# Memory projections in three rounded passes inside an attention pipeline, with VectorE's share placed in ScalarE's filling step

## The reference

```
h = RMSNorm(x);  z = h @ w_in                 # 2048 x 5944, columns shared out among two mixers
y_a = native sparse attention of z            # 8 heads of 128, 2 key/value groups
      k_cmp, v_cmp: gelu(blocks @ w1) @ w2    # 15 blocks of 32 tokens: 4096 -> 128 -> 128
y_b = RWKV-7 of z                             # 16 heads of 64
x  += concat(RMSNorm(y_a), y_b) @ w_out
m   = RMSNorm(mem);  k = m @ wk_mem;  v = m @ wv_mem       # both 2048 x 2048
x  += attention(RMSNorm(x) @ wq_mem, k, v) @ wo_mem
x  += hierarchical mixture of experts (4 groups of 8, top 2)
out = RMSNorm(x)
```

## Time and profile before

| | |
|---|---|
| runs | 1944.14, 1943.7, 1938.69 us; median 1943.7 |
| the profiled execution | 1943.37 us, its span 1941.5 us |
| busy share of the span | PE 91%, DVE 48%, ACT 34%, POOL 4% |
| mean granted TensorE clock | 0.946 of 2.4 GHz |
| the chain that ended last | PE 89%, DVE 4%, ACT 3% |
| L683 and L672 in the chain (float32 products of all units) | 20.3% and 7.4% |

### The profile page before, as it was taken

How to read it: one execution, slowest core, us unless ns; L and a number is a source line. 1 busy time by engine, 2 the same in 40 slices (tenths; PEclk the granted TensorE clock), 3 DMA queues, 4 the chain that set the end, 5 groups by cost and what they waited for, 6 DMA issues and landing times.

```text
span 1941.5 us, 28278 instructions
## 1 busy us (share of the span) xinstructions
PE 1774.4 (91%) x11978; PEld 1526.5 (79%) x11978; DVE 941.5 (48%) x1119; ACT 665.9 (34%) x709; POOL 72.6 (4%) x150
## 2 busy tenths in 40 slices
PE   6999999999989999969879789669999999998993
PEld 4887878878788888869879689668877886886882
DVE  1142423434223111143443334448878878887883
ACT  1011111101111111132333323236765765765772
POOL 4010010101010000000000000000000000000000
PEclk9899999999969999989989999769999998999997
DMA  7430605133126444416525153239977987995972
GB/s 204 143 106 9 207 11 172 53 109 115 45 94 213 131 130 130 130 69 191 173 87 177 39 164 124 87 121 360 380 302 270 378 309 267 378 372 204 380 300 109
DMA packets 173374, 351.55 MB, mean 181 GB/s; under 512 B 12707, under 2 KB 145388, under 8 KB 147436
## 3 DMA queue, kind: packets, MB, share of 16 engines
q1 hardware_dynamic: 173292, 350.33, 51.4%
HBM read 348.22 MB, written 2.10 MB: 180 GB/s over the span
## 4 chain that ended last, share of the span: by engine, by line
PE 89%; DVE 4%; ACT 3%; issue 1%; POOL 1%; DMA 1%; SPq 0%; DVEq 0%; ACTq 0%; POOLq 0%
PE bank L683 20%; PE bank L1114 18%; PE bank L999 10%; PE bank L1133 9%; PE bank L672 7%; PE bank L1003 5%; PE bank L1079 2%; PE bank L898 1%; PE bank L787 1%; PE bank L704 1%; PE bank L802 1%; PE bank L1100 1%; PE bank L797 1%; PE bank L1037 1%; ACT split L1425 1%
## 5 line engine op out<-in xcount | busy, mean ns | idle before, releaser
L1878 DVE TENSOR_TENSOR split<-weights_raw,split 128x2048 fp32r<-128x2048 f32 x192 | 439.0, 2292 | 90.0 <-ACT split L1425 87.0
L683 PE MATMUL bank<-arena_fixed 128*128 128x256 f32 x1792 | 414.3, 386 | 0.0
L1425 ACT CAST split<-weights_raw 128x2048 fp32r<-128x2048 f32 x192 | 367.0, 1914 | 121.9 <-PE bank L1114 73.3
L683 PEld LDWEIGHTS bank<-arena_fixed 128*128 128x128 f32 x1792 | 334.9, 191 | 53.9 <-issue 8.3
L1114 PE MATMUL bank<-split,gathered_hi 128*128 128x512 f32 x1024 | 323.1, 397 | 13.8 <-DVE split L1878 9.3
L1114 PEld LDWEIGHTS bank<-split,gathered_hi 128*128 128x128 f32 x1024 | 191.3, 190 | 53.8 <-issue 10.0
L1114 PE MATMUL bank<-split,gathered_lo 128*128 128x512 f32 x512 | 201.8, 394 | 0.0
L999 PE MATMUL bank<-loop_split,act_over_hT 128*128 128x256 f32 x768 | 166.7, 286 | 7.7 <-DVE act_over_concat L1719 7.7
L1133 PE MATMUL bank<-split,hidden_hi 128*128 128x512 f32 x512 | 163.3, 401 | 5.3 <-DVE hidden_lo L1917 5.3
L999 PE MATMUL bank<-loop_split,act_over_concat 128*128 128x256 f32 x768 | 165.6, 285 | 2.8 <-DVE act_over_hT L1773 2.8
L1726 DVE TENSOR_TENSOR loop_split<-arena_fixed,loop_split 128x2048 fp32r<-128x2048 f32 x48 | 107.8, 2288 | 84.3 <-ACT loop_split L1354 84.3
(11 more groups left out here) (353 smaller groups left out, 1791.9 us busy)
## 6 DMA issues: line engine op xcount, KB each, us to landing
weights_raw<-in_moe_w_gate_dram SPq DMA_DIRECT2D x64, 1024.0 KB, 5.1
weights_raw<-in_moe_w_up_dram SPq DMA_DIRECT2D x64, 1024.0 KB, 7.1
weights_raw<-in_moe_w_down_dram SPq DMA_DIRECT2D x32, 2048.0 KB, 7.6
arena_fixed<-in_w_in_dram SPq DMA_DIRECT2D x22, 2048.0 KB, 8.2
arena_fixed<-in_wk_mem_dram SPq DMA_DIRECT2D x8, 2048.0 KB, 8.9
arena_fixed<-in_wv_mem_dram SPq DMA_DIRECT2D x8, 2048.0 KB, 8.6
arena_fixed<-in_w_out_dram SPq DMA_DIRECT2D x8, 2048.0 KB, 8.7
arena_fixed<-in_wq_mem_dram SPq DMA_DIRECT2D x8, 2048.0 KB, 8.6
```

The lines of the kernel that those rows point to most:

```text
L683: mm = pe.matmul(b[:, half * T:half * T + T], w[:, c, half * P:half * P + P], hT[:, c, :], start=st, stop=en)
L1425: nc.scalar.copy(split_half(i, 0, j), raw_half(j, hf)).then_inc(act_hi, 1)
L1878: V.tensor_tensor(split_half(i, 1, j), raw_half(j, hf), split_half(i, 0, j).bitcast(F32), ALU.subtract)\
```

## The change

Four things are done at once.

**Split memory weights.** The memory units no longer go through the ring's float32 products. Each unit is loaded into slot 0 or 1 and cut in 4 quarters ("pieces", 64 in all, 8 products each). ScalarE rounds a quarter (hi), VectorE subtracts (lo), both into one of six buffers (`NPB`), and TensorE multiplies in three passes. The normed memory is split as well (`mem_split`, `split_nm`). ScalarE rounds a quarter as soon as TensorE has read the one six before it (`piece_read`). A unit of v starts with one matmul of zeros over its bank.

**The order of the filling.** `Filling` gives all three engines the same steps. 8 products come before the `w2` products, 8 behind them, then 11 in each gap. In a step ScalarE rounds the quarters whose buffers TensorE frees in that very step, and VectorE, which had no filling before, subtracts the same quarters in the same step: behind "m" of pair i and ahead of "p" of pair i-1.

**Turned compression.** `blk` is stationary (32 columns, two of them zero) and `w1` moves (128 columns), four partial sums on four quarters of the output partitions. ScalarE copies these, and one more small product with `sel` adds the four. GpSimd builds `blk` before its work for the last RWKV group.

**Moved.** The norm of `mem` is computed within the last RWKV group, its transposes run before the compression. The units of q move: the groups have 4, 5, 5 and 5 units.

```diff
-        nsa_order = [[("q", 0), ("q", 1)], [("q", 2), ("q", 3)], [("kc", 0), ("vc", 0)],
-                     [("ks", 0), ("kw", 0), ("vs", 0), ("vw", 0)]]
+        nsa_order = [[("q", 0)], [("q", 1), ("q", 2)], [("kc", 0), ("vc", 0)],
+                     [("q", 3), ("ks", 0), ("kw", 0), ("vs", 0), ("vw", 0)]]
...
         FILL2 = 11
+        EARLY2 = 8
+        GAPS2 = [EARLY2, EARLY2] + [FILL2 for i in range(NHT + 2)
+                                    for _ in range((i < NHT) + (0 < i <= NHT) + (i > 1))] + [8 * PIECES]
+            def step(self):
+                old, self.at = self.at, min(self.at + next(self.gaps), 8 * PIECES)
+                return old, self.at
...
+            for n, (key, i) in enumerate(mem_units):          # SyncE
+                if n == 0:
+                    sp.wait_ge(*pe_proj.at(proj[-1]))
+                elif n == 1:
+                    sp.wait_ge(*pe_n.at(("nm", 7)))
+                else:
+                    sp.wait_ge(piece_lo, 4 * (n - 2) + 4)
...
+            norm_transposes("nm", mem_slot, 8)                # TensorE
             pe.wait_ge(*pool_a.at("blk"))
...
-                for l in range(CMP):
-                    mm = pe.matmul(bank[2 + i][:, 0:2 * NCMP], w1[:, l, :], blk[:, i, l, :],
-                                   start=l == 0, stop=l == CMP - 1)
+                for l4 in range(CMP // 4):
+                    for j in range(4):
+                        l = 4 * l4 + j
+                        mm = pe.matmul(bank[2 + i][32 * j:32 * j + 32, 0:P], blk[:, i, l, :], w1[:, l, :],
+                                       start=l4 == 0, stop=l4 == CMP // 4 - 1)
             mm.then_inc(*pe_a.mark("h"))
-            norm_transposes("nm", mem_slot, 8)
-            pe.wait_ge(*dve_n.at(("nm", "out", 7)))
+            pe.wait_ge(*act_a.at("hcw"))
+            for i in range(2):
+                mm = pe.matmul(bank[2][:, P + 32 * i:P + 32 * i + 32], hcw[:, i, :], sel, start=True, stop=True)
+            mm.then_inc(*pe_a.mark("sum"))
+            PASSES = ((0, 0), (0, 1), (1, 0))
...
+            def mem_product(k):
+                n, r = divmod(k, 2 * NC)
+                key, p = mem_units[n], k // 8
+                b = bank[(len(proj) + n) % 2]
+                if r == 0:
+                    pe.wait_ge(*act_proj.at((proj + mem_units)[len(proj) + n - 2]))
+                if k == 0:
+                    pe.wait_ge(*dve_ml.at(7))
+                if k % 8 == 0:
+                    pe.wait_ge(piece_lo, p + 1)
...
+                    for t, (x_, w_) in enumerate(PASSES):
+                        mm = pe.matmul(b[:, half * T:half * T + T], pieces[p % NPB][:, w_, at:at + P], mem_x(x_, c),
+                                       start=c + t == 0, stop=c == NC - 1 and t == 2)
+                if k % 8 == 7:
+                    mm.then_inc(piece_read, 1)
...
+            def mem_weights(p):                               # ScalarE
+                n, i = divmod(p, 4)
+                if i == 0:
+                    act.wait_ge(mem_full[n % 2], 16 * (n // 2 + 1))
+                if p >= NPB:
+                    act.wait_ge(piece_read, p - NPB + 1)
+                nc.scalar.copy(piece_half(p, 0), raw_piece(p)).then_inc(piece_hi, 1)
+            def gap2():
+                old, new = filling.step()
+                for p in range(old // 8, new // 8):
+                    if p + NPB < PIECES:
+                        mem_weights(p + NPB)
+                    if p % 4 == 3:
+                        mem_out(p // 4)
...
+            def mem_weights(p):                               # VectorE
+                dve.wait_ge(piece_hi, p + 1)
+                V.tensor_tensor(piece_half(p, 1), raw_piece(p), piece_half(p, 0).bitcast(F32), ALU.subtract)                    .then_inc(piece_lo, 1)
+            def gap2():
+                last = filling.step()[1] // 8
+                for p in range(done[0] + NPB, min(last + NPB, PIECES)):
+                    mem_weights(p)
+                done[0] = last
```

More of the change, by code:

```diff
@@ L50 @@
 MRAW = 3
+NPB = 6
+PW = 1024
 SPLITS = 3
@@ L168, in decoder_layer @@
         Us = r1.take(2, CH)
+        blk_at = -(-r1.at // 32) * 32
+        r1.at = blk_at
+        blk = r1.take(2, CMP, 32)
+        hcw = r1.take(2, P)
+        sel = r1.take(32)
+        zer = over("zeros", r1.at, P)[:, :]
+        r1.take(P)
         r2 = Region(nsa_end, ARENA)
@@ L323, in decoder_layer @@
             fill_of.append(list(range(first, len(units))))
+        units.append(("mem", "mem", 0))
         units.append(("w1k", "w1", 0))
         units.append(("w1v", "w1", 1))
-        units.append(("mem", "mem", 0))
         wkm = wk_mem[0].rearrange("(c p) n -> p c n", p=P)
         wvm = wv_mem[0].rearrange("(c p) n -> p c n", p=P)
[L329 to L337, removed]
+        mem_units = [("mk", i) for i in range(8)] + [("mv", i) for i in range(8)]
+        NMU = len(mem_units)
+        PIECES = 4 * NMU
         index = {k: i for i, (k, _, _) in enumerate(units)}
@@ L340, in decoder_layer @@
         NLU = D // UC
-        n_before = loop_first + NLU * len(LOOPS)
-        assert index["mem"] % RING == MEM_SLOT
+        assert index["mem"] % RING == MEM_SLOT and len(units) % RING == 0
         NLT = NLU * len(LOOPS)
@@ L346, in decoder_layer @@
         ring_full = [sem(f"ring_full{s}") for s in range(RING)]
+        mem_full = [sem(f"mem_weights_full{s}") for s in range(2)]
+        piece_hi, piece_lo, piece_read = sem("piece_hi"), sem("piece_lo"), sem("piece_read")
         moe_full = [sem(f"moe_raw_full{s}") for s in range(MRAW)]
@@ L903, in _ @@
+            def gap2():
+                for k in range(*filling.step()):
+                    mem_product(k)
+            gap2()
             pe.wait_ge(*dve_a.at("gelu"))
             pe.wait_ge(s_w2, 32)
[L905 removed]
+            pe.matmul(bank[3][:, 0:2 * NCMP], w2[:, 0, :], hc[:, 0, 0:2 * NCMP], start=True, stop=True)
             for g in range(NG):
[L907 removed]
+                mm = pe.matmul(bank[3][0:NCMP, P + g * P:2 * P + g * P], hc[:, 1, g * NCMP:g * NCMP + NCMP], w2[:, 1, :],
@@ L1716, in _ @@
                         .then_inc(*dve_a.mark(("p", i - 1)))
+                    gap2()
+                if i > 1:
+                    gap2()
+            gap2()
+            for p in range(done[0] + NPB, PIECES):
+                mem_weights(p)
             def activations_lo(dst, src, hi, o, count):
@@ L2017, in _ @@
                 link(G_.tensor_copy(id64[r], ident[r, r]))
+            G_.tensor_copy(sel, ident[:, 0:32])
+            G_.memset(zer.bitcast(F32), 0.0)
+            for i in range(2):
+                G_.memset(blk[:, i, :, 2 * NCMP:], 0.0)
             link(G_.memset(reset, 1.0))
+            for j in range(1, 4):
+                link(G_.tensor_tensor(sel, sel, ident[:, 32 * j:32 * j + 32], ALU.add))
             rv = reset.rearrange("p (c t) -> p c t", t=CH)
```

182 lines of the change are left out of this document (117 added, 65 removed).

## The result

The changed kernel takes 1960.62 us (median of 5 runs, 1958.14 to 1963.89), the kernel before 1944.14 (5 runs, 1938.69 to 1947.91): ratio 1.0081, interval 1.0061 to 1.0101. It is slower by 0.8%. The forecast was 1947 us, range 1930 to 1968. The profiled execution took 1963.89 us (span 1962.4), 20.5 more than the one before; 16.9 us more than forecast are to be found.

A forecast was written before the change was run, and what follows sets the result against it. TensorE alone was taken to bound the memory stage. Terms of -41.5, +2, -25, +2, +51.6 and +0.5 gave -10.4 us, or +3.6 with the clock's +14: from 1943.4 to 1947 us, range 1930 to 1968.

The forecast's parts named there:

- the side with the highest chance: Whole kernel: slower than 1949.5 us, chance 0.43, against 0.20 for faster and 0.37 for the same.
- the rival of the lost clock: Memory stage: clock lost behind nearly every transposes wait, 1968 us; chance 0.21 together with an unpacked compression.
- +3.6 us: Whole kernel: the sum of all forecast terms with the clock's loss included; without it -10.4 us.
- The products (-41.5): Memory products on TensorE: three split passes take 0.359 us a product instead of 0.440, saving 41.5 us over 512.
- The zeros (+2): Memory products on TensorE: eight matmuls of zeros with 512 columns cost below 2 us.
- Ahead of the stage (-25, +2): Last projection to first memory product: 18.3 us instead of 43.3; first 8 products at half clock cost 2.
- The waits (+51.6): Memory stage: TensorE waits for VectorE's late "p" at fourteen transposes, plus delays of "m" and the start, 51.6 us.
- The clock (+14): Memory stage: seven of fourteen waits lose TensorE's full clock at 2 us each; bounds 0 and 43.
- The tail (+0.5): End of the memory stage: the 16 early products are missing from the last steps, exposing about 0.5 us.
- VectorE's place costs nothing: Memory stage: rival in which the 47 us of waits and the clock's 14 go, 1886 us; chance 0.06.
- The clock holds: Memory stage: rival with the same waits, but only the longest two or three lose the clock, 1937 us; chance 0.20.
- No gain in the passes: Memory products: rival in which the three split passes bring no gain, the 41.5 us go, 1988 us; chance 0.03.

The follow-up runs named there:

- e7: Changed kernel with VectorE's subtractions one gap behind ScalarE, and quarters 2 and 3 subtracted before the wait for the `w2` products: 1883.92 us, ratio 0.9701 to the kernel before.
- e4: Changed kernel with the compression unturned (`w1` stationary, 32 columns of `blk` moving, no sum of four parts): 1984.45 us, ratio 1.0189 to the kernel before.
- e1: Changed kernel with VectorE's subtractions of the gap behind the scores moved behind the scaling "p": 1895.43 us, ratio 0.9743 to the kernel before.
- e3: Changed kernel with 20 useless matmuls added ahead of the transposes of each pair but the last: 1946.41 us, ratio 1.0012 to the kernel before.

## Why the prediction was right, and where it was not

The time fell into the range and on the side with the highest chance. But 1960.6 is nearer to the rival of the lost clock (1968) than to the forecast (1947). That it is slower was carried by the chances, not by the sum: +3.6 us is within the 5.8 that the text itself called no change, and +16.5 was measured. The waits were foreseen by their cause; that the total still fell into the range owes something to the range's width. The terms one by one:

*The products (-41.5).* Undisturbed, the products, of three matmuls in two rows of the timeline, start 0.36 us apart, as forecast:

```profile
580.77 0.40 PE L976 MATMUL bank<-mem_hi_low_chunks,piece 128*128 128x256 f32 x2
...
581.13 0.40 PE L976 MATMUL bank<-mem_hi_low_chunks,piece 128*128 128x256 f32 x2
```

But a gap of 33 takes 4.05 us instead of 3.95: over the 45 gaps that is +4.5 us. The rate was read from a loop in which nothing but such matmuls run, and a gap stands between small float32 matmuls; that this is the reason was not tried. The zeros (+2) were not measured apart.

*Ahead of the stage (-25, +2).* The chain has it, in answer to the earlier trace rows:

```profile
552.33 3.67 PE bank L938 x128
...
562.77 5.46 PE bank L976 x24
568.24 0.24 PE bank L988 x2
568.48 0.55 PE bank L990 x4
```

The transposes took 5.1 us (547.2 to 552.3) as forecast (the row from which 0.111 was read, L960, is one of value products, not of transposes, of the same size); the compression 3.67, not 5, which is 0.029 us a matmul, the lower bound of "four at once"; the stretch behind it 6.8 where 7.3 were forecast; the first 24 matmuls 5.46 us at half clock against 2.9, so 2.6 for the 2. In all 1.3 us better than forecast.

*The waits (+51.6).* 52.7 us in 14 waits, none in step 15, each released by L1850, and "p" stood behind exactly the chain m, e, rounding, subtraction that the text had added up. The lengths that it built on are those of the page (quarters of 1.22 and 1.03 us were forecast):

```profile
L1787 DVE TENSOR_TENSOR piece<-arena_fixed,piece 128x1024 fp32r<-128x1024 f32 x64 | 77.8, 1223 | 158.1 <-ACT piece L1387 158.1
...
L1387 ACT CAST piece<-arena_fixed 128x1024 fp32r<-128x1024 f32 x64 | 66.2, 1042 | 74.3 <-PE bank L976 37.7
```

Of step 14, with two quarters in its gap, the timeline says 4.16 us for a forecast of 3.6; of step 5, with one, 2.84 for 2.9. Step by step, what the text adds up to is within 0.6 us of the timeline in steps 3 to 14, so the total is not right by large errors that cancel; only steps 1 and 2 are over, by 1.3 and 1.2. That odd steps wait longer than even ones did not show: 3.3 us in the mean of steps 3 to 13 against 3.5 in steps 2 to 14. The waits stand at L1020; L1005, which the text names, is the scores. The first wait is near in size and not right in kind: 8.66 us where the text has the odd step's 2.9 and 4.5 for the start, 1.7 of them at scores that never waited. The text named VectorE's eight quarters as the reason for the start, and called the load of 2 MB hidden. It is not hidden: it is issued by the very subtractions that the change puts late, and e7 shows that this was what remained.

*The clock (+14): the step that failed.* The mechanism was right and the size was not: the term took seven falls of 14 at 2 us. There were 13, at the price it had read from the earlier trace rows: 1.9 us, so 24.7 us instead of 14, +10.7. It had reckoned by the length of a wait: from one that kept the clock after 2.76 us and one that lost it after 2.8, it took it that about half would fall. Length does not decide it alone, as the timeline shows (in brackets the idle time ahead and its releaser):

```profile
784.87 0.45 PE L1020 MATMUL bank<-arena_fixed,arena_phases 128*128 128x128 f32 x2 [3.16 <-DVE arena_phases L1850]
...
821.48 0.69 PE L1020 MATMUL bank<-arena_fixed,arena_phases 128*128 128x128 f32 x2 [2.61 <-DVE arena_phases L1850]
```

```profile
782.00:784.00 2.00, 0.00 (x0) 1.00 0.35 115
...
821.00:823.00 2.00, 1.52 (x7) 0.50 0.00 0
```

The wait of 3.16 us kept the clock and that of 2.61 lost it. e4 shows it better still. Its 14 waits at the transposes are those of the changed kernel within 0.01 us, but for the first (8.27), and yet its trace has 11 falls and not 13: its waits of 3.25 us (ended at 747.58) and 2.60 us (842.45) kept the clock, where those of 3.25 and 2.61 had lost it.

```profile
747.00:749.00 2.00, 1.42 (x12) 1.00 0.02 6
...
843.00:845.00 2.00, 2.00 (x20) 1.00 0.00 0
```

Over all waits at the transposes in the nine changed traces: none of up to 1.95 us lost the clock, 16 of the 22 from 2.19 to 3.25 us did, and all 20 that were longer. What decides in between stays open. For about eight falls on the text itself expected a slower kernel ("It decides from about eight falls on"); there were 13, and it is slower.

*The tail (+0.5).* Ahead of the last pair's value products (L1034) TensorE is idle for 0.45 us behind ScalarE's copy of the output before it, and the eight matmuls then take 1.13 us instead of 0.89: 0.7 in all for 0.5.

The sum of the misses is 4.5 - 1.3 + 1.1 + 10.7 + 0.2 = 15.2 us, and with 1.6 us outside of both stretches 16.8, of the 16.9 that were to be found. The falls are 10.7 of them. Two small slips stand in the text's own figures: with no fall and a compression of 3.6 us its sum gives 1943.4 - 10.4 - 1.4 = 1931.6, not 1934, and its shares for "slower" add up to 0.44, not 0.43.

*The rivals.* "VectorE's place costs nothing" is refuted by e1. "The clock holds" is refuted by the 13 falls. "No gain in the passes" is refuted by e7: TensorE is busy for 230.9 us in the stage where it was 261.8, 30.9 less. The terms give 41.5 - 4.5 (the gaps' length) - 2 (zeros) - 2.6 (start at half clock) - 0.8 (the `w2` products, now inside the stage) = 31.6. The rival of the lost clock had the number of falls nearly right (14 for 13) and, at 2.5 us, too high a price for one.

## What to carry to other kernels

Ask of every piece of filling work what stands behind it in its engine's list and who waits for that: the same instructions, put behind the scaling instead of ahead of it, gave 65 us back. Where a wait of some three microseconds or more returns in each step, as here, count a fall of the clock for nearly each instead of for half of them, at a price read from the matmuls behind an idle stretch. And when a subtraction frees the slot of the next load, its place also sets when that load starts.

## What the runs showed of the hardware

- Waits of 2.6 to 4.2 us, some 20 us apart, cost TensorE's full clock in 12 of 13 cases in the changed kernel and in 10 of 13 in e4, where they are as long; 1.6 to 2.0 us each beside the wait itself. In about half of the cases the clock fell only when work was there again. Cut to 1.3 us in the mean (e3), they cost it once in all, in the one of 5.7 us; no wait of up to 1.95 us did.
- Useless matmuls in such a wait pay: 300 of them made the kernel 14 us faster; where there was no wait to fill, they made it 27 us slower.
- 128 float32 matmuls with a stationary tile of 32 columns on four quarters of the output partitions ran in 3.67 us, 0.029 us each, against 0.111 for one of 128 columns alone: nearly four times. The Trainium skill (TensorEngine Tiling (Array Packing), Theoretical Speedup) gives up to four times for a dimension of at most 32; the trace agrees.
- With 32 moving columns and a weight load of 128 for each, TensorE was busy in all of 22 us and its clock stayed at 1.2 GHz, to which it had fallen within the first microsecond of this work (e4). Being busy did not bring the clock.
